# Hybrid SSD / gMLP / attention encoder on one core: chunk decays with the column term summed by TensorE and one exponential of 512 columns

## The reference, cut to what matters

```
acs = cumsum(dt * a_neg)                       # per chunk and head
seg = acs[t] - acs[s]
decay_in = exp(where(tri, seg, NEG_INF))       # 128 x 128 per head and direction
y_diag = einsum(cb, decay_in, xdt)             # cb = C B^T, per group
states = einsum(bc, decay_out, xdt)            # then a scan over the chunks
y = y_diag + y_off + d_skip * x ;  y = rmsnorm_by_group(y * silu(z))
```

## Time and profile before

| | |
|---|---|
| median of 3 runs | 2511.89 us (2510.75 to 2516.29) |
| the profiled execution | 2516.7 us, span 2514.9 us |
| granted TensorE clock, mean over the span | 0.99 |
| PE busy | 2438.0 us (97%) |
| PEld busy | 2079.7 us (83%) |
| DVE busy | 1373.1 us (55%) |
| ACT busy | 997.8 us (40%) |
| POOL busy | 1256.5 us (50%) |
| chain that ended last | PE 83%, DVE 7%, ACT 4%, issue 2%, DMA 2%, POOL 1% |

### The profile page before, as it was taken

The page is one execution under the profiler, slowest core; times in us unless marked ns, Lnnn a source line. Parts: engine busy times, 40 slices in busy tenths (PEclk is TensorE's granted clock), DMA queues, the critical chain, the costliest instruction groups (busy, mean ns, idle before and its releaser), DMA issues.

```text
span 2514.9 us, 32967 instructions
## 1 busy us (share of the span) xinstructions
PE 2438.0 (97%) x12882; PEld 2079.7 (83%) x12882; DVE 1373.1 (55%) x1561; ACT 997.8 (40%) x1737; POOL 1256.5 (50%) x814
## 2 busy tenths in 40 slices
PE   7999999899999999998999999998999999999999
PEld 7989997787788888787899899977877888887887
DVE  3476657738555555337244765576385546543442
ACT  4345558613444443202024456585144444431110
POOL 3232114224877777566633321142248877866664
PEclk9999999999999999999999999998999999999999
DMA  4534443221222222643332334442212212226444
GB/s 158 134 117 126 133 157 128 94 94 67 84 84 84 84 82 76 241 143 117 126 134 74 119 126 138 147 139 88 84 67 101 84 67 101 76 94 224 142 142 142
DMA packets 102964, 290.68 MB, mean 116 GB/s; under 512 B 7800, under 2 KB 30328, under 8 KB 101112
## 3 DMA queue, kind: packets, MB, share of 16 engines
q1 hardware_dynamic: 80360, 255.73, 30.0%
q10 hardware_dynamic: 22456, 32.90, 4.0%
HBM read 229.84 MB, written 58.75 MB: 115 GB/s over the span
## 4 chain that ended last, share of the span: by engine, by line
PE 83%; DVE 7%; ACT 4%; issue 2%; DMA 2%; POOL 1%; ACTq 0%; SPq 0%; DVEq 0%; POOLq 0%
PE PS L689 21%; PE PS L693 20%; PE PS L692 20%; PE PS L774 3%; PE PS L778 3%; PE PS L777 3%; PE PS L944 2%; DMA RAW<-wst 2%; PE PS L933 2%; DVE ACC L1735 1%; PE PS L1080 1%; PE PS L1115 1%; PE PS L923 1%; ACT LG L1487 1%; PE PS L922 1%
## 5 line engine op out<-in xcount | busy, mean ns | idle before, releaser
L604 POOL CAST WH<-RAW 128x1024 fp32r<-128x1024 f32 x156 | 179.2, 1149 | 933.3 <-PE PS L689 343.1
L689 PE MATMUL PS<-HH,WH 128*128 128x512 f32 x1264 | 499.2, 395 | 7.3 <-DVE UU L2249 7.0
L693 PE MATMUL PS<-HH,WL 128*128 128x512 f32 x1264 | 495.5, 392 | 0.0
L692 PE MATMUL PS<-HL,WH 128*128 128x512 f32 x1104 | 432.7, 392 | 0.0
L606 POOL TENSOR_TENSOR WL<-RAW,WH 128x1024 fp32r<-128x1024 f32 x156 | 395.6, 2536 | 12.5
L689 PEld LDWEIGHTS PS<-HH,WH 128*128 128x128 f32 x1264 | 238.8, 189 | 60.5 <-issue 7.7
L689 PE MATMUL PS<-AR,WH 128*128 128x512 f32 x704 | 277.5, 394 | 7.8 <-POOL WL L606 6.0
L693 PEld LDWEIGHTS PS<-HH,WL 128*128 128x128 f32 x1264 | 238.6, 189 | 52.3
L693 PE MATMUL PS<-AR,WL 128*128 128x512 f32 x704 | 276.8, 393 | 0.0
L692 PE MATMUL PS<-AR,WH 128*128 128x512 f32 x704 | 276.2, 392 | 0.0
L2228 DVE TENSOR_TENSOR AR<-ARL,AR 128x512 fp32r<-128x512 f32 x88 | 134.8, 1575 | 242.6 <-ACT AR L1672 242.6
(11 more groups left out here) (274 smaller groups left out, 4644.0 us busy)
## 6 DMA issues: line engine op xcount, KB each, us to landing
RAW<-wst SPq DMA_DIRECT2D x156, 512.0 KB, 3.4
TOE<-toe_d SPq DMA_DIRECT2D x64, 512.0 KB, 3.8
act_d<-CVV SPq DMA_DIRECT2D x22, 1024.0 KB, 4.0
ARL<-act_d SPq DMA_DIRECT2D x88, 256.0 KB, 3.1
RAW<-wst SPq DMA_DIRECT2D x20, 1024.0 KB, 4.9
RAWB<-wst SPq DMA_DIRECT2D x20, 1024.0 KB, 4.9
XBS<-xbc_d SPq DMA_DIRECT2D x24, 512.0 KB, 4.1
xbc_d<-CV ACTq DMA_DIRECT2D x16, 512.0 KB, 3.6
```

Source lines behind the costliest of these rows:

```text
L604: nc.gpsimd.tensor_copy(hi, raw).then_inc(hi_done, 1)
L689: ins = nc.tensor.matmul(out, wh, xh, start=first, stop=False, skip_group_check=onto)
L692: nc.tensor.matmul(out, wh, xl, start=False, stop=False, skip_group_check=onto)
L693: return nc.tensor.matmul(out, wl, xh, start=False, stop=last, skip_group_check=onto)
```

## The change

The column term is no longer ACT's bias. A second table `NRM` holds the transposed `NACS` (16 directions and heads by 4 chunks on 64 partitions, a copy of it below for a low half), and `SID` is the folded identity that picks four of its rows. `sums` gets a third product, `NRM` times four columns of `SID`, each repeated 128 times, and ACT takes one exponential of 128x512 without a bias where it took four of 128x128. The table is filled by four small products in `bias_rows()` (PE, at i == 2 of the reverse pass), one ACT copy of 128x256 (at i == 3), and two DVE instructions in `far()`, one of 128x64 and one of 64x256. Nothing else moves.

```diff
--- before.py
+++ after.py
@@ -266,6 +266,8 @@
         SEG1 = place("SEG1", [P, 4, 4, P], u_at)
         YN = place("YN", [P, 2, INNER], u_at + 20480)
         ZG = place("ZG", [P, 2, 3, UC], u_at + 8192)
+        NRM = place("NRM", [P, 2, P], u_at + 24576, F32R)
+        SID = place("SID", [P, 64], u_at + 25600, F32R)
         JUNK = place("JUNK", [P, GROUPS, 256], u_at + 16384)
         XBS = place("XBS", [P, 2, XBC_T, P], u_at + 49184)
         XBR = place("XBR", [P, 2, XBC_T, P], u_at)
@@ -1017,6 +1019,16 @@
                                                 start=True, stop=True, skip_group_check=True)
                     last.then_inc(rows_full, 1)
 
+                def bias_rows():
+
+                    pe.wait_ge(att_done, (l + 1) * NT)
+                    for part in range(2):
+                        for low in range(2):
+                            last = nc.tensor.matmul(PS[low * 64:low * 64 + 64, 7, (2 + part) * P:(3 + part) * P],
+                                                    NACS[:].rearrange("p c e -> p (c e)")[:, part * 64:part * 64 + 64],
+                                                    ident, start=True, stop=True, skip_group_check=True)
+                    last.then_inc(rows_full, 1)
+
                 def tile_in(i):
                     pe.wait_ge(xbs_full[i % 4], 16 * (l * (6, 6, 2, 1)[i % 4] + i // 4 + 1))
 
@@ -1041,6 +1053,8 @@
                     pe.wait_ge(ra_t_full, l * LINKS + i + 1)
                     pe.sem_inc(xbs_used, 1)
                     ra_state(i - 1)
+                    if i == 2:
+                        bias_rows()
 
                 def chunk_turn(i2, par):
                     for j in range(6):
@@ -1061,8 +1075,11 @@
                         part, c = divmod(n % NT, 4)
                         rows = c * 4 + d * 2 + g
                         nc.tensor.matmul(bank(2 + j % 2), SEL[:, rows:rows + 1].to_broadcast((P, P)),
-                                         MHL[:, part].rearrange("p h n -> p (h n)"), start=False, stop=True,
-                                         skip_group_check=True).then_inc(ab_full, 1)
+                                         MHL[:, part].rearrange("p h n -> p (h n)"), start=False, stop=False,
+                                         skip_group_check=True)
+                        nc.tensor.matmul(bank(2 + j % 2), NRM[:, part],
+                                         SID[:, 4 * rows:4 * rows + 4].unsqueeze(2).to_broadcast((P, 4, P)),
+                                         start=False, stop=True, skip_group_check=True).then_inc(ab_full, 1)
 
                 def chunk(i2, par, end):
                     c = i2 * 2 + par
@@ -1545,7 +1562,7 @@
                         A(IDR[:], ident, ACT.Copy)
                         A(SEL[:], fours, ACT.Copy)
                         A(GRP[:], fourth, ACT.Copy)
-                        act.wait_ge(rows_full, l + 1)
+                        act.wait_ge(rows_full, 2 * l + 1)
                         for h in range(4):
                             last = A(MHL[:, :, h, :], PS[:, 6, 0:2 * P].rearrange("p (a n) -> p a n", a=2), ACT.Copy,
                                      scale=fourth[:, h:h + 1])
@@ -1554,6 +1571,9 @@
                             rows = slice(64 * low, 64 * low + GG)
                             last = A(BST[rows], PS[rows, 6, 2 * P:3 * P], ACT.Copy)
                         last.then_inc(far_step, 1)
+                    if i == 3:
+                        act.wait_ge(rows_full, 2 * l + 2)
+                        A(NRM[:].rearrange("p a n -> p (a n)"), PS[:, 7, 2 * P:4 * P], ACT.Copy).then_inc(far_step, 1)
                     if 1 <= i <= 4:
                         for t in range(2):
                             gate_square(2 * i - 2 + t)
@@ -1590,15 +1610,10 @@
                         act.wait_ge(sf_full, l * LINKS + c)
                     A(BC[:].rearrange("p a g n -> p (a g n)"), bank(1), ACT.Copy).then_inc(bst_ready, 1)
                     for j in range(4):
-                        g, d = divmod(j, 2)
                         act.wait_ge(ab_full, 1 + n * 4 + j + 1)
                         if j == 0:
                             act.wait_ge(yd_full, n + 1)
-                        for h in range(4):
-                            e = d * 8 + g * 4 + h
-                            last = A(SEG[par][:, j, h, :], PS[:, 2 + j % 2, h * P:(h + 1) * P], ACT.Exp,
-                                     bias=NACS[:, c, e:e + 1])
-                        last.then_inc(exp_ready, 1)
+                        A(SEG[par][:, j].rearrange("p h n -> p (h n)"), bank(2 + j % 2), ACT.Exp).then_inc(exp_ready, 1)
                         if j == 1:
                             v_scaled(c)
                     if c < LINKS:
@@ -2060,7 +2075,10 @@
                 def far():
                     for d, tri in enumerate((tri_f, tri_b)):
                         TS(FAR[:, d, :], tri, 1.0, 1e30, ALU.subtract, ALU.mult)
-                    dve.wait_ge(far_step, l + 1)
+                    dve.wait_ge(far_step, 2 * l + 2)
+                    TT(SID[:], ident[:, 0:64], ident[:, 64:P], ALU.add)
+                    TT(NRM[64:P].rearrange("p a n -> p (a n)"), PS[64:P, 7, 2 * P:4 * P],
+                       NRM[64:P].rearrange("p a n -> p (a n)").bitcast(F32), ALU.subtract)
                     TT(BST[64:64 + GG], PS[64:64 + GG, 6, 2 * P:3 * P], BST[64:64 + GG].bitcast(F32), ALU.subtract)
                     for h in range(4):
                         low = MHL[64:P, :, h, :]
```

## The result

The changed kernel takes 2544.3 us (median of 4, 2541.8 to 2544.84) against 2514.09 us (median of 4, 2510.75 to 2517.29) of the kernel before: 1.2% slower, ratio 1.0118 with a 95% interval of 1.0101 to 1.0136. The forecast was slower, 2536 us, with a range from 2518 to 2542: right in sign and in the turns of POOL and DVE, but 8 us short, and the time lies 2.3 us above the range. The sum held no cost for the clock, which came to 5.0 us in the chunks of the profiled execution. The profiled execution has a span of 2543.0 us, 28.1 more than before.

A forecast was written before the change was run, and what follows sets the result against it. PE was taken to bound the kernel, interrupted by DVE's decay mask. Chunks 1 to 6 21.8, chunk 0 2.0 and setup 1.8 summed to 25.6, taken as 24: 2536 us, range 2518 to 2542.

The forecast's parts named there:

- PE sets the pace, ACT's relief is worth nothing by itself: Middle chunks: PE limits; added products cost 0.93 us per chunk, ACT's 2.1 us given back gain nothing by themselves.
- ACT at some 37 us busy of 53: Chunk stage window: a sign that the forecast is right, ACT's busy time falling from 48.77 us to some 37.
- POOL and DVE take turns, and `Y2` comes just early enough for two turns inside the masks: Chunk stage masks: Y2 starts 0.63 us earlier, POOL's L659 falls into group 0's L2128; the chunk takes 10.54 us.
- Chunks 1 to 6: Both layers: six chunks at 10.54 us, 63.2 against 52.75 and 51.91, cost 21.8 us.
- The turn rule of the prediction: DVE instructions with two SBUF operands and POOL's don't overlap; whoever waits gets the next turn, about 0.55 or 1.13 us.
- Chunk 0: First chunk of each layer: 9.6 us against 8.65, costing 1.0 us per layer, 2.0 in all.
- Setup: Reverse pass: bias_rows 0.4 us on the chain of states, far() on DVE 0.5; 0.9 per layer, 1.8 in all.
- The clock stays up: Chunk stage: the sum held no cost for a lower clock after PE's new idle of 1.1 us per chunk.
- rival D: Chunk stage: the clock falls after PE's new idle, once more per layer; +5 us, 2541 us, chance 0.07.
- The base: Whole kernel: the forecast was carried to the median of 2511.89 us, adding 24 us.

The follow-up runs named there:

- e1: Changed kernel, with POOL's addition of Y2 to Y3 also waiting until both mask products of the chunk are done; 2524.26 us, ratio 1.0038.
- e7: Kernel before, with POOL adding Y1 to Y3 before it waits for Y2; 2512.31 us, ratio 0.9990.
- e3: Changed kernel with its third product, but ACT again takes four exponentials of 128x128, without a bias; 2538.72 us, ratio 1.0094.
- e6: Changed kernel, with ACT doing the squares of the chunk before ahead of Y2 instead of after it; 2528.56 us, ratio 1.0063.
- e8: Changed kernel, with POOL adding Y1 to Y3 before it waits for Y2; 2535.07 us, ratio 1.0087.
- e10: The changed kernel itself, measured a second time; 2541.7 us, ratio 1.0109.
- e5: Changed kernel, with four unused 128x512 products filling PE's wait before the second half of L1115 in chunks 1 to 6; 2540.64 us, ratio 1.0108.
- e11: The kernel of e5 measured again, side by side with e10; 2540.03 us, ratio 1.0104.
- e4: Changed kernel without the third product of the sums, so its decays lack the column term; 2540.73 us, ratio 1.0105.

## Why the prediction was wrong, step by step

1. *PE sets the pace, ACT's relief is worth nothing by itself.* Right. ACT's 30 us are gone and no period of the changed kernel fell below those of before. e1 shows the period with the third product and without turns in the masks, 9.20, and e7 that without the product, 8.34: the product costs 0.86 us per chunk, 0.93 forecast. The prediction set 0.25 us per 128 columns against 0.48 for 512 as what a longer instruction saves; by e3 most of that difference goes with the bias operand. Its sign "ACT at some 37 us busy of 53" was wrong: it is 30.00, since 53 us now hold about five chunks and not six.
2. *POOL and DVE take turns, and `Y2` comes just early enough for two turns inside the masks.* Right in place and size: 10.51 us per chunk against 10.54 forecast. A chunk of the mean period 8.79 before (first layer) becomes 10.51: +0.86 for the product, +1.31 for the turns (10.51 - 9.20), -0.45 for what the kernel before already lost to turns (8.79 - 8.34). Chunks 1 to 6 at full clock: 6 x 10.51 = 63.06 against 52.75 and 51.91, 21.5 us; 21.8 forecast. The turn rule of the prediction, taken from four rows and one case in the FFN, also gives the rows of e3, e6 and e8, and in e1, where no request falls into the masks, they last 0.69 us. The GPSIMD Engine Reference of the Trainium skill (section Key points) names the contention only; the order of turns is what decided here.
3. *Chunk 0.* It took 8.65 and 8.54 us and now takes 9.92 and 9.56: 1.27 and 1.02 more, 2.3 us against 2.0.
4. *Setup.* Mis-sized. From the first state product to the first L1080 it was 402.95 - 386.79 = 16.16 us, and is now 403.91 - 386.54 = 17.37; the second layer has nearly the same difference (1.23). That is 2.4 us for both instead of 1.8. The state product behind `bias_rows` started 391.42 - 388.62 = 2.80 us after the one before, not 2.06: the whole 0.74 us lay on the chain, of which I had taken 0.4. I had expected the idle time of 0.30 us before it to take up a part; it is still there, now ended by the transposes at L994 ahead of it:

```profile
388.62 1.10 PE L1005 MATMUL PS<-XWA,BSTA 128*128 128x256 f32 x4 [0.30 <-DVE BW L2101]
391.42 1.10 PE L1005 MATMUL PS<-XWA,BSTA 128*128 128x256 f32 x4 [0.30 <-PE PS L994]
```

5. *The clock stays up (rival D beside the sum, chance 0.07).* This is the step that failed: the sum had no term for the clock. Three of the twelve chunks ran with a stretch at half clock and took 12.2 us instead of 10.51: 3.4 us in the first layer and 1.7 in the second, 5.0 in all (3.4 in the execution of e10). The trace of before had shown both the long waits and the half-clock stretch after them; I named the new idle of 1.1 us per chunk, but kept its cost as a rival instead of a term, without a reason for putting it at nothing. My 5 us for it came from a stretch as long as the one of before, once per layer; that it met the 5.0 is in part luck. e5 and e11 show that the idle is what it hangs on. The other kernels agree: e1 and e6, with no idle time noted there, have no such chunk, e8 with 0.9 us has one, e3 with 1.10 two, and e4 with 1.53 four.
6. *The base.* The forecast was added to 2511.89 us, three runs. With one more run before stands at 2514.09. And I put 24 for a sum of 25.6.

In the span, 2.4 + 2.3 + 21.5 + 5.0 = 31.2 us were added up to chunk 7 of both layers, and 28.1 are measured. From the first L1080 of chunk 7 to the first L727 of the output projection (L1097 and L729 in the changed kernel) the first layer took 23.44 us and now takes 21.02, the second 25.31 and now 23.41: 4.3 us less in all. In the first layer 2.1 of it is the clock: the kernel before ran the first products of the output projection at the lower level (481 to 486 us in the earlier trace rows) and took 6.61 us up to L727 (481.18 to 487.79), and the changed one took 4.51 (496.76 to 501.27) at the full level. In the second, the kernel before waited 2.71 us for the first mask of chunk 7, the changed one 1.44. The 1.2 us that are then missing (31.2 - 4.3 is 26.9) lie elsewhere in the program and I don't assign them. With the clock as a term and the measured base, the prediction's own sum is 2514.1 + 25.6 + 5 = 2545; that it comes so near is in part luck, since neither the 4.3 us nor the 1.2 us stand in it.

Still open: which chunk loses the clock. In the first layer it was chunks 1 and 6 in one execution of the changed kernel and chunk 3 in another (e10), and chunk 5 in e3 with the same periods, though the chunks are alike. What PE's idle must amount to before the clock falls isn't shown either.

## What to carry to other kernels

Where two engines take turns, the moment at which an instruction asks decides what it costs: here an addition that became ready 0.7 us earlier in the chunk cost more than the work that was saved. Before you make an off-path engine faster, write down what it triggers, in whose middle that now falls, and what the triggered engine has queued behind it. A wait that holds the trigger back until the other's pair is done is worth a try first: here one line was worth 17 to 20 us to the changed kernel, and one reordering with one such wait 7 us to the kernel before. An idle time that a change makes on PE can have two prices, its own length and what the lower clock costs after it; both belong in the sum.

## What the runs showed of the hardware

A per-partition bias costs ACT time: eight exponentials of 128x128 out of PSUM took 2.17 us with it and 1.47 us without (e3), 0.09 us each. ScalarE: Activation LUTs of the Trainium skill (section What ACT_TABLE_LOAD costs) states about 93 ns for each such operand; the trace agrees. One exponential of 128x512 against four of 128x128, both without bias, saved only 0.1 to 0.2 us (two last 1.08 to 1.27 us in the changed kernel, eight 1.46 to 1.47 in e3).

A moving operand whose columns are one element repeated 128 times costs PE no more than its neighbour without the repetition: 433.50 - 433.28 = 0.22 us for 512 columns, against 433.28 - 433.05 = 0.23.
